# Encoder layer with cross-attention: one ones-product for each softmax sum and each norm statistic, and a new order

## The reference

```python
n2 = rmsnorm(h, g_cross[l])
mn = rmsnorm(mem, g_mem[l])
xq = (n2 @ w_xq[l]).reshape(b, s, N_X_HEADS, X_HEAD_DIM)      # 4 heads of 256
xk, xv = ...                                                  # from mn @ w_xkv, 256 memory tokens
sc = jnp.einsum('bshd,bmhd->bhsm', xq, xk).astype(jnp.float32) * (X_HEAD_DIM ** -0.5)
pr = jax.nn.softmax(sc, axis=-1).astype(xv.dtype)
h = h + jnp.einsum('bshd,bmhd->bshd', pr, xv).reshape(b, s, d) @ w_xo[l]
n3 = rmsnorm(h, g_ffn[l])
h = h + jnp.square(jax.nn.relu(n3 @ w_ff1[l])) @ w_ff2[l]
```

## Time and profile before

| | |
|---|---|
| time, median of 3 runs | 2193.19 us (2193.01 to 2197.26) |
| profiled execution, its own time | 2199.46 us |
| its span, slowest core | 2197.5 us (cores 2176.4 to 2197.5) |
| TensorE busy | 2122.5 us, 97% |
| VectorE busy | 1644.3 us, 75% |
| ScalarE busy | 1387.5 us, 63% |
| GpSimd busy | 352.0 us, 16% |
| DMA, share of 16 engines | 66.4%, 470 MB |
| chain that ended last | TensorE 77%, DMA 9%, VectorE 4%, ScalarE 4%, issue 4% |

### The profile page before, as it was taken

How to read it: one execution, slowest core, us unless ns; L and a number is a source line. 1 busy time by engine, 2 the same in 40 slices (tenths; PEclk the granted TensorE clock), 3 DMA queues, 4 the chain that set the end, 5 groups by cost and what they waited for, 6 DMA issues and landing times.

```text
span 2197.5 us, 37323 instructions; the slowest of 8 cores (2176.4 to 2197.5 us)
## 1 busy us (share of the span) xinstructions
PE 2122.5 (97%) x12311; PEld 1063.2 (48%) x12474; DVE 1644.3 (75%) x2323; ACT 1387.5 (63%) x1731; POOL 352.0 (16%) x271
## 2 busy tenths in 40 slices
PE   9889998989999999999999999999999999999998
PEld 5433333434345644456444753465445644475457
DVE  5776887777777797778978778778777787877563
ACT  6787787647865578545785468546764478546431
POOL 1222323111221023101210020101120021001200
PEclk9999999999999999999999999999999999999999
DMA  8978987899697874558734673357534763467355
GB/s 246 307 248 245 311 287 249 280 298 321 202 281 238 285 251 154 166 182 275 241 116 134 212 267 126 129 187 240 184 122 150 256 208 108 138 216 261 127 161 194
DMA packets 152394, 472.52 MB, mean 215 GB/s; under 512 B 17040, under 2 KB 21264, under 8 KB 152208
## 3 DMA queue, kind: packets, MB, share of 16 engines
q1 hardware_dynamic: 152208, 470.14, 66.4%
HBM read 399.82 MB, written 70.25 MB: 214 GB/s over the span
## 4 chain that ended last, share of the span: by engine, by line
PE 77%; DMA 9%; DVE 4%; ACT 4%; issue 4%; SPq 1%; POOL 0%; DVEq 0%; ACTq 0%; POOLq 0%
PE ps L739 77%; DMA M_p<-wst 6%; ACT M_p L1213 2%; DMA wsc<-W_p 2%; SPq L747 1%; ACT W_p L759 1%; DMA wsc<-M_p 1%; DVE M_p L1224 1%; DVE M_p L852 0%; SPq L751 0%; DVE S_p L1418 0%; DVE W_p L1527 0%; DVE M_p L1225 0%; ACT M_p L826 0%; DVE M_p L968 0%
## 5 line engine op out<-in xcount | busy, mean ns | idle before, releaser
L739 PE MATMUL ps<-S_p,W_p 128*128 128x512 bf16 (+1 forms) x5337 | 1059.2, 351 | 13.4 <-issue 2.4
L739 PEld LDWEIGHTS ps<-S_p,W_p 128*128 128x128 bf16 x5440 | 519.7, 98 | 533.5 <-issue 82.5
L1213 ACT ACTIVATE M_p<-ps 128x2048 bf16<-128x2048 f32 x256 | 479.5, 1873 | 275.2 <-PE ps L739 265.8
L739 PE MATMUL ps<-M_p,W_p 128*128 128x256 bf16 (+1 forms) x3607 | 624.4, 327 | 10.7 <-ACT W_p L759 6.2
L739 PEld LDWEIGHTS ps<-M_p,W_p 128*128 128x128 bf16 x3656 | 350.8, 98 | 270.8 <-issue 45.2
L1224 DVE TENSOR_TENSOR M_p<-M_p 128x1024 f32<-128x1024 f32 x216 | 274.6, 1272 | 120.4 <-ACT M_p L1213 116.4
L1225 DVE TENSOR_TENSOR M_p<-M_p 128x1024 f32<-128x1024 f32 x216 | 274.0, 1269 | 13.1 <-DVE M_p L1224 0.5
L1471 ACT ACTIVATE M_p<-M_p 128x512 bf16<-128x512 f32 x256 | 158.1, 627 | 174.1 <-DVE M_p L1469 173.9
L835 POOL TENSOR_TENSOR M_p<-M_p 128x512 f32<-128x512 f32 x79 | 112.6, 1427 | 941.2 <-ACT M_p L826 900.6
L1469 DVE SCALAR_TENSOR_TENSOR M_p<-ps,M_p 128x512 f32<-128x512 f32 x256 | 174.6, 687 | 86.7 <-PE ps L739 78.7
L826 ACT ACTIVATE M_p<-M_p 128x512 f32<-128x512 f32 x216 | 130.3, 624 | 93.0 <-DVE M_p L1429 45.0
(11 more groups left out here) (89 smaller groups left out, 1757.1 us busy)
## 6 DMA issues: line engine op xcount, KB each, us to landing
W_p<-wsc SPq DMA_DIRECT2D x490, 512.0 KB, 4.8
M_p<-wst SPq DMA_DIRECT2D x182, 512.0 KB, 10.1
wsc<-W_p SPq DMA_DIRECT2D x76, 512.0 KB, 9.4
M_p<-xT SPq DMA_DIRECT2D x120, 256.0 KB, 6.9
outT<-M_p SPq DMA_DIRECT2D x56, 256.0 KB, 5.4
n1d<-M_p SPq DMA_DIRECT2D x28, 256.0 KB, 6.5
M_p<-n1d SPq DMA_DIRECT2D x28, 256.0 KB, 6.4
pdd<-M_p SPq DMA_DIRECT2D x14, 256.0 KB, 6.8
```

Of the source, the lines that this page charges most:

```text
L739: return e.matmul(out(), lhsT=lhsT(), rhs=rhs(), start=start, stop=stop, skip_group_check=True, **kw)
L1213: A(lambda e: e.activation(out=b16(P).rearrange("p (a n) -> p a n", n=512), in_=ps[:, 0:4, :], func=AF.Exp, scale=0.125), 2048, True, S, [P])
```

## The change

It does four things.

1. `norm_step` adds a head's two probability tiles on VectorE (a bf16 addition into a new S1 tile, `xPs`) and makes one ones-product of the sum.
2. `stat_after` uses `group = 8`: all eight squares of s2 and of s3 are added in f32, and one ones-product follows.
3. The planner's assumed costs change: GpSimd's operations become cheaper, VectorE's charge for the port it shares with GpSimd falls, results of TensorE are assumed ready earlier.
4. Stretches of side work and the seed of the jitter change, so the whole order is drawn again.

```diff
-           (query(*blocks[1]), ("o2", 0.0), ("o2", 0.2)), (attention(*blocks[1]), ("o2", 0.22), ("F0", 0.97))]
+           (query(*blocks[1]), ("o2", 0.0), ("o2", 0.2))]
...
-PE_TAIL = 175.0
+PE_TAIL = 110.0
...
+SHARE1 = ((34, ('o2', 0.37), ('F0', 0.928)),)
+QUERY = (0.07, 0.46)
...
-SEED, JITTER = 2, 60.0
+SEED = 3616
+JITTER = 60.0
...
-        return 0.0 if b == "pe" else 160.0
+        return -PE_TAIL if b == "pe" else 160.0
...
-            return 300.0 + n * 2.1
+            return 300.0 + n * 1.9
...
-            return G.op((("dve", dve_t(n) + 30.0), ("pool", pool_t(n))), fn, R, W, port=True)
+            return G.op((("dve", dve_t(n) + 5.0), ("pool", pool_t(n))), fn, R, W, port=True)
...
-            cost = dict(act=act_t(n, psum, scale is not None), dve=dve_t(n, rate), pool=200.0 + n * 1.1)
+            cost = dict(act=act_t(n, psum, scale is not None), dve=dve_t(n, rate), pool=200.0 + n * 0.85)
...
-                group = 4
+                group = 8
...
-                    b = V("xss", "D")
-                    PE([mm(lambda: ap(b), lambda: ones[:], lambda mt=mt: ap(P[mt]), mt == 0, mt == 1, [CONST["ones"], P[mt]])
-                        for mt in range(2)], [b])
+                    b, both = V("xss", "D"), V("xPs", "S1")
+                    D(lambda e: e.tensor_tensor(out=ap(both), in0=ap(P[0]), in1=ap(P[1]), op=ALU.add), 512, P, [both], rate=2.0, port=True)
+                    PE([mm(lambda: ap(b), lambda: ones[:], lambda: ap(both), True, True, [CONST["ones"], both])], [b])
```

More of the change, by code:

```diff
@@ L58, in AUX @@
     aux = [(attention(*blocks[0]), ("o1", 0.0), ("o1", 1.0)),
-           (query(*blocks[1]), ("o2", 0.0), ("o2", 0.2)), (attention(*blocks[1]), ("o2", 0.22), ("F0", 0.97))]
+           (query(*blocks[1]), ("o2", 0.0), ("o2", 0.2))]
+    steps, k = attention(*blocks[1]), 0
+    for n, lo, hi in SHARE1:
+        part, k = steps[k:k + n], k + n
+        aux.append((part, lo, hi))
     for b in range(2, 8):
-        aux.append((query(*blocks[b]), (f"A{b - 1}", 0.0), (f"A{b - 1}", 0.5)))
+        aux.append((query(*blocks[b]), (f"A{b - 1}", QUERY[0]), (f"A{b - 1}", QUERY[1])))
         steps, k = attention(*blocks[b]), 0
@@ L83 @@
 LEAD0 = 4
-SHARE = ((6, ("A", 0.6), ("B", 0.0)), (6, ("B", 0.0), ("F", 0.0)), (6, ("F", 0.0), ("F", 0.53)), (16, ("F", 0.53), ("F", 0.97)))
-TILES = ((("F1", 0.0), ("F1", 0.45)), (("A2", 0.1), ("F2", 0.0)), (("F2", 0.0), ("F2", 0.45)), (("A3", 0.0), ("A3", 0.6)))
+SHARE = ((6, ('A', 0.7), ('B', 0.0)), (6, ('B', 0.0), ('F', 0.0)), (6, ('F', 0.0), ('F', 0.53)), (16, ('F', 0.53), ('F', 0.97)))
+SHARE1 = ((34, ('o2', 0.37), ('F0', 0.928)),)
+QUERY = (0.07, 0.46)
+TILES = ((('F1', 0.0), ('F1', 0.51)), (('A2', 0.1), ('F2', 0.0)), (('F2', 0.0), ('F2', 0.65)), (('A3', 0.26), ('A3', 0.7)))
 NORM1 = (1, 4)
@@ L728, in D @@
         def D(fn, n, R, W, rate=1.0, ptr=0, port=False):
-            return G.op((("dve", dve_t(n, rate) + 50.0 * ptr + 60.0 * port),), fn, R, W, port=port)
+            return G.op((("dve", dve_t(n, rate) + 50.0 * ptr + 5.0 * port),), fn, R, W, port=port)
         def TT(fn, R, W, n=512):
-            return G.op((("dve", dve_t(n) + 30.0), ("pool", pool_t(n))), fn, R, W, port=True)
+            return G.op((("dve", dve_t(n) + 5.0), ("pool", pool_t(n))), fn, R, W, port=True)
         def mm(out, lhsT, rhs, start, stop, R, n=512, mode="f", tile=None, half=False):
```

## The result

| | before | changed |
|---|---|---|
| time, median (runs) | 2195.23 us (2193.01 to 2197.54, 4 runs) | 2168.49 us (2165.83 to 2225.41, 4 runs) |
| profiled execution, its span | 2199.46 us, 2197.5 us | 2170.98 us, 2169.4 us |

In one execution of the changed kernel (2225.41 us) the cores of one die ran at a lower granted clock, and all ratios of this document leave such executions out. The ratio is 0.9874, with a 95% interval of 0.9855 to 0.9893. That is 27.7 us less, between 23.5 and 31.8. The forecast was 13.3 us less. The direction is right, the time lies inside the range, and the size is twice what the sum gave. The range of 2166 to 2192 us holds by luck in part: on the base that the forecast used, 2193.19 us, the same ratio gives 2165.6 us.

The account below looks back on a forecast made before the run. TensorE was taken to bound the late stretch; early it also waits for weights still landing. Products -10.4, fillers -2.3, early holds -1 and latency +0.4 made -13.3 us, from 2193.19 to 2180 us, range 2166 to 2192.

Parts of the forecast that it names:

- The products: TensorE's stream: 48 fewer sums with ones at 0.216 us each, 10.4 us less, lower end 9.1.
- The added work: VectorE and GpSimd: 32 bf16 additions, 13 us, and 16 f32 additions, 13 to 23 us, hidden behind TensorE.
- Latency of the last block: Block 7, between last scores and output product: the head's addition lies on the path once, +0.4 us.
- the cover: TensorE work hiding the additions' latency before the ones-product; if gone in every block, 3.4 us, the upper end.
- The fillers: Planned products of ones in TensorE's gaps: 22 fewer, 2.3 us less, with 0 and 4.8 as ends.
- The early holds: Early stage, weight casts holding the softmax Exp and TensorE: 4.5 us a hold, -1 us taken, bounds -9 to +18.
- the 8 us that I allowed: Before 550 us: TensorE's waits behind Exp should stay within 8 us of 17.2.
- the 17.2 us behind Exp scale with the casts in front of it as 11/81: ScalarE's queue before 550 us: fewer weight casts there cut TensorE's waits by 2.3 us, GpSimd's casts taking back part.
- A: TensorE's stream: removed products and fillers come back as waits; 2192 us, no change; chance 0.15.
- B: Up to 550 us: 90 GpSimd casts free staging tiles later and hold the Exp; slower, 2199 us; chance 0.07.
- C: Early stage: the new order makes early holds all but vanish, 10 us beyond the forecast, 2170 us; chance 0.16.
- the forecast's own range of 2172 to 2187: Whole kernel: range around 2180 us with the bounds of fillers and early holds narrowed to one hold either way.

Follow-up runs that it names:

- e1: Changed kernel, order unchanged on every engine, each of the 48 sums with ones issued twice in a row; ratio to the kernel before 0.9910.
- e4: Changed kernel, order unchanged, without the 75 planned fillers behind 700 us; ratio to the kernel before 0.9874.
- e13: Changed kernel with seed 1290 in place of 3616, the earliest end of plan among 2400 seeds; ratio to the kernel before 0.9872.
- e3: Changed kernel with both product edits undone, keeping its planner prices, stretches and seed; ratio to the kernel before 0.9996.
- e11: Changed kernel with only TensorE's planner price of before and seed 24, an average drawing; ratio to the kernel before 0.9968.
- e5: Changed kernel with seed 2, that of before, in place of 3616; ratio to the kernel before 0.9941.
- e9: Changed kernel with the stretches of side work (start positions) of before, prices and seed as changed; ratio to the kernel before 0.9927.
- e6: Changed kernel with seed 7 in place of 3616; ratio to the kernel before 0.9897.
- e10: Changed kernel with seed 2163 in place of 3616, a bad drawing by the planner's list; ratio to the kernel before 1.0046.
- e7: Changed kernel with all planner prices of before, seed 3616 and stretches as changed; ratio to the kernel before 1.0048.
- e12: Changed kernel with the GpSimd and shared-port prices of before, TensorE's as changed, seed 21, an average drawing; ratio to the kernel before 1.0003.
- e2: Kernel before with the two product edits alone; prices, stretches and seed as before, order drawn again; ratio to the kernel before 0.9984.

## Why the prediction was right in direction and short in size

**The products: right.** 48 x 0.216 = 10.4 us was forecast; the rest column falls by 10.5, and e1 gives them back at 10.6 in a fixed order. Late too they count in full. VectorE's first instruction of line 1469 in a block (1476 in the changed kernel, 1478 in e1), the relu behind the first feed-forward products, tells when core 1 has got there (blocks 1 and 7 before, then of the changed kernel, then of e1; first and last start behind the durations):

```profile
L1469 DVE SCALAR_TENSOR_TENSOR M_p<-ps,M_p x32: 677/688/693, 606.0 to 680.9; 128x512 f32<-128x512 f32 x32
...
L1469 DVE SCALAR_TENSOR_TENSOR M_p<-ps,M_p x32: 679/691/692, 2075.7 to 2126.1; 128x512 f32<-128x512 f32 x32
```

```profile
L1476 DVE SCALAR_TENSOR_TENSOR M_p<-ps,M_p x32: 674/684/692, 593.1 to 665.1; 128x512 f32<-128x512 f32 x32
...
L1476 DVE SCALAR_TENSOR_TENSOR M_p<-ps,M_p x32: 682/692/692, 2045.5 to 2095.9; 128x512 f32<-128x512 f32 x32
```

```profile
L1478 DVE SCALAR_TENSOR_TENSOR M_p<-ps,M_p x32: 673/683/693, 599.0 to 671.9; 128x512 f32<-128x512 f32 x32
...
L1478 DVE SCALAR_TENSOR_TENSOR M_p<-ps,M_p x32: 680/691/692, 2059.8 to 2110.2; 128x512 f32<-128x512 f32 x32
```

Against the kernel before, block 1 is 12.9 us earlier (606.0, now 593.1) and block 7 is 30.2 (2075.7, now 2045.5): 17.3 us over six blocks, 2.9 a block, where I forecast some 2. In the mean of the eight cores the gain is 9.3 us up to block 1 and 16.2 from there to block 7, so the larger part lies late. The six sums of a block are 1.3 us of it, 7.8 in six blocks. e1 prices these by themselves: from block 1 to block 7 it takes 1460.3 us in the mean of the eight cores and the changed kernel 1453.0, 7.3 us for the 36 products. What a block gained beyond the sums, some 1.4 us, is mostly fillers: between block 1 and block 7 they go from 92 to 61, 6.7 us.

**The added work: right, and more of it on GpSimd.** The 32 additions have a median of 418 ns (forecast 417 from the earlier trace rows). TensorE waited 1.7 us for them, in four places. Latency of the last block: 5.16 us with three sums against 5.62 with six before; without the sums 4.51 against 4.32, so +0.2 where I took +0.4. The statistics' additions grew by the 16 of the sum, but GpSimd took 22 more of them and VectorE 6 fewer (core 1), so GpSimd gained 70.9 us, outside my 20 to 50, and VectorE 28.6 instead of 15 to 25 (65 and 25.5 us in the mean of the eight cores). Behind 600 us TensorE waited 0.5 us for line 1421, and the cover held.

**The fillers: mis-sized, and wrong in kind.** I took half of 22 x 0.216 as gain, because no row told what a gap would be without its fillers. e4 does for the late ones: it would be a gap. So a filler is not a term beside the waits but part of them, and the only question was whether the new order has the gaps. Late it has not: 23 fillers fewer, 5.0 us, at the same idle time. That is the upper end, 4.8, and not the 2.3 of the sum.

**The early holds: there, but far too small.** The waits behind Exp fell by 11.5 us up to 550 us on the slowest core, outside the 8 us that I allowed, and by 12.4 us in the mean of all cores over the whole span. With the other waits, the fillers and the clock it is 14.0 us; my three terms for this (fillers, holds, latency) made 2.9. Of the 14.0, 5.7 lie late, above all the fillers, 1.1 are clock, and 7.2 lie early, where the sum had 1. The step that was mis-sized most is "the 17.2 us behind Exp scale with the casts in front of it as 11/81", with GpSimd's casts taking back part. The count was right: casts of f32 weight halves on ScalarE went from 81 to 70. What one is worth was not. GpSimd's casts took nothing back: in the mean of the cores the Exps waited 3.5 us for them before and 0.2 us now, though there are 14 more. For ScalarE's own, twelve different orders were profiled (casts on ScalarE, and the waits behind Exp in us, mean of eight cores):

| | changed | e13 | e3 | e11 | e5 | e9 | e6 | e10 | before | e7 | e12 | e2 |
|---|---|---|---|---|---|---|---|---|---|---|---|---|
| casts | 70 | 70 | 71 | 75 | 76 | 77 | 78 | 79 | 81 | 82 | 82 | 84 |
| waits | 8.4 | 10.7 | 7.1 | 15.2 | 17.9 | 10.7 | 13.0 | 14.1 | 20.8 | 16.3 | 21.6 | 26.8 |

A straight line through the twelve has a slope of 1.0 us for each cast (correlation 0.84), about the 1.05 us that such a cast lasts; it reaches zero waits at 62 casts. My proportion gave 17.2 / 81 = 0.21. So it looks as if the casts that an order has above some 62 are those that land in front of an Exp that is due, and each holds it for its own duration, or more where its load is late. That is a correlation over orders which differ in other ways too; no run moved a single cast, so the cause is argued and not shown. Nor do these waits tell the time: over the twelve orders they go with the ratio at a correlation of 0.44 only, the column of waits with fillers at 0.90. Why the new order holds less, early and late, stays open.

How long ScalarE sits idle in front of its casts does not explain it either. On core 1 it is 76.6 us in e2, 52.9 before and 42.4 in the changed kernel, but 52.6 in e1 and 63.4 in e4, which have the changed kernel's order on ScalarE and its short waits behind Exp.

**How the 27.7 us divide.** The products make 10 to 10.6 (e1), and the order the other 17. Of the order, the choice of 3616 over a typical seed makes 14.7 (0.9941 less 0.9874, e5, known to some 5 us). All new prices together are worth 23.5 us against e5 (e7), and one by one 5.9 and 13.6 (e11, e12). With the products these sum to 45 to 49 us and not to 27.7: e7, with the changed products, the old prices and another seed, is 10.5 us slower than the kernel before instead of 10 faster. Luck explains part of it. By the planner's own lists the kernel before is a good drawing of its prices, 4.6 us ahead of the mean of 120 seeds (20 of them end earlier), and e7 a poor one, some 4 us behind its own. Some 12 us are left over, by either way of pricing. Each ratio is known to some 4 us, and e7, e11 and e12 all have the new stretches, which may be what goes badly with the old prices; no run separates these. Which of the prices and stretches brought what stays open, and so does what a cut of 32 products in the order of the kernel before would give, which wasn't run.

**The rivals.** A is excluded by e1, and e2 looks like it from outside. B, Exps held by GpSimd's casts, did not happen: 90 casts on GpSimd, no wait of TensorE on any core is put down to GpSimd, and the Exps wait for its casts at most 0.8 us on a core (2.0 to 4.9 before). C, that the order helps more than I count, is nearest in number: 14.4 us beyond the forecast where C had 10. But C placed it in the early holds, and 5.7 of the 12.9 us lie late. It had a chance of 0.16, against 0.62 for the forecast's own size. Five seeds now show that a replanned order alone moves the time by up to 38 us, and nothing in the profile of before bounds that; the forecast's own range of 2172 to 2187 was too narrow.

## What to carry to other kernels

Where a planner with a random seed writes the order, an A/B of two programs compares two drawings as well: price an edit with the order held fixed (issue the removed work twice), and give the replanned order a term of its own with the scatter of a few seeds. It was 38 us here between the best and the worst, the worst having been picked to be bad; between e5 and e6, which were not, it was 10 us. Within one set of prices the end of the planner's list ranked the drawings (e5, e6, e10, e13), across prices it did not: the list of e3 ends 19 us ahead of that of the kernel before, and both take the same time. Count fillers and idle time as one quantity. A proportion to the number of instructions in front of a wait is no price for it: here it was a fifth of the slope that twelve orders show.

## What the runs showed of the hardware

- One of the 32 bf16 additions took 1257 ns, three times the median of 418, where line 1488 had at most 665 ns before. A GpSimd cast had begun 0.49 us ahead of it, and it ends 0.28 us behind that cast's end. Time line of the changed kernel:

```profile
309.88 1.47 POOL L769 CAST W_p<-M_p 128x1024 bf16<-128x1024 f32 x1 [4.51 <-DMA M_p<-wst]
310.37 1.26 DVE L1421 TENSOR_TENSOR S_p<-S_p 128x512 bf16<-128x512 bf16 x1
```

  By the rule of the Trainium skill that the prediction weighed ("SBUF — State Buffer", Who interferes with whom: the second to start waits for the first) it would run its 0.42 us behind the cast's end, at 311.35; it took 0.28, so this one meeting agrees within the accuracy of GpSimd's spans.
- In the mean VectorE and GpSimd run a little longer in the new order; that meetings like this are the cause was not tested. TensorE waited 1.7 us in all for the new additions. VectorE's additions of line 1232 (1225 before) have a mean of 1333 ns on core 1, where it was 1282, and GpSimd's of line 842 (835 before) one of 1500, where it was 1434; GpSimd has 37 instructions more. The changed kernel's rows:

```profile
L1232 DVE TENSOR_TENSOR M_p<-M_p 128x1024 f32<-128x1024 f32 x216 | 288.0, 1333 | 12.0 <-DVE M_p L1231 0.5
...
L842 POOL TENSOR_TENSOR M_p<-M_p 128x512 f32<-128x512 f32 x113 | 169.3, 1500 | 866.9 <-ACT M_p L833 846.0 <-DVE M_p L842 13.6 <-POOL M_p L842 5.9
```

- Late fillers do a little besides covering waits: without 75 of them the clock's loss rose from 7.8 to 11.3 us, and core clocks fell to 0.994 to 0.997 from 0.995 to 0.997.
- Eight cores that run one program differ by 11 to 22 us in the profiled executions (12.8 in the changed kernel, 22.4 in e11) and by 7 to 25 us in all that the ratios use, and which core is slowest changes from execution to execution. The difference arises early: in the kernel before, block 1's first relu lies between 594.7 and 616.0 us, and from there to block 7's all eight cores take 1466.8 to 1470.6 us.
